# Router of a hybrid layer: experts chosen in two batches of token tiles

## The chip, the cores and the metric

One core of one Trainium2 chip runs the kernel. The metric is the device time in microseconds of one execution; lower is better. All times of instructions are microseconds from the start of the span.

## The reference, cut to what matters

One layer over 512 prompt tokens and 32 sample tokens, width 1024: a pooling branch and a differential attention are merged and projected, `x = x + merged @ w_out`, and then a mixture of experts is added. The change is in how the experts are chosen and how the token lists of each expert are made:

```
g_logits = t @ w_router_group + b_router_group          # 4 groups
g_sel = argmax(g_logits); g_w = softmax(g_logits)[g_sel]
e_logits = (t @ w_router_expert + b_router_expert)[g_sel]  # 4 experts of that group
top_v, top_i = top_k(e_logits, 2); top_w = softmax(top_v) * g_w
y += combine[:, e] * (silu(t @ w_gate[e]) * (t @ w_up[e])) @ w_down[e]     # 16 experts
```

Here `t` is the row-normalised `x`.

## The kernel before, in words

Each engine has its own queue, written out by hand; semaphores join them. Products of fp32 accuracy are made of three products of split operands (`wh`/`wl` high and low parts, in four slots), lines 1767 to 1769.

The 544 tokens are five tiles of 128 (`NT = 5`; index 0 to 4 is tile 0, 1, 2, 4, 3; the tile with the sample tokens comes fourth and is short). The output projection runs in ten steps `s`: steps 0 to 4 make the left 512 columns of the five tiles, 5 to 9 the right ones. For each step VectorE adds the result to `x` (`add_half`, lines 1485 to 1488, semaphore `o_ev`), ScalarE squares it (line 996), the tensor engine turns it (`turn_half`, line 2123), ScalarE copies the turned half (line 1003), and the tensor engine makes the half's 20 logits per token (`logits_half`, line 2131, semaphore `lg_mm`). For steps 5 to 9 ScalarE also takes the root of the row's mean square (line 1008), VectorE its reciprocal (line 1494) and the normalised rows `hb` (`normal_rows`, line 1503), which POOL sends to memory (lines 619, 621).

Logits of the left halves are copied from bank 6 into `lg`; those of the right halves are added out of bank 7, in one go for the first four tiles (lines 1527 to 1529) and apart for the last (1540, 1541). Then VectorE chooses: `first_max` (lines 1547 to 1551) three times, for the group, the first and the second expert, over all five tiles, 4 or 16 values per token, 19 chained instructions in all (each waits for the one ahead of it by `link`). `sel_done` starts 5 products on the tensor engine that count how many tokens ahead of each one chose the same expert (lines 2182, 2184), and 5 more for the totals (2188). VectorE meanwhile makes list values `oht` (1565, 1566) and the rows of the last tile, and then the place of each token in its expert's list (1570 to 1576) and one-hots over the 128 slots (`slot_hot`, 1578). Ten products make the lists (2194); line 1589 turns them into row numbers `idi`, POOL gathers the first experts' rows (595), and they are turned (2214) and split (ScalarE 1020, VectorE `xl` 1688). Behind line 1589 VectorE makes further list columns (1591), the weights (1597 to 1604), `item_w` (1609), the other list ids (1616) and `tail_lists` (1621 to 1629), which is used at the end of the kernel only. From `item_w` ten products (2281) make the weights of the slots; they stand in the tensor engine's queue directly ahead of the first expert's products.

The expert weights come in chunks of 512 KB, 24 slots `rawM`; ScalarE makes `wh` (989) and VectorE `wl` (`m_lo_split`, 1509, later 1642) of each. The first two chunks are split by VectorE between the last halves, the third after `xl`. Between its tasks in the router the tensor engine runs `idle_products`, filler that nobody reads (line 2138), in counts from the tuple `IDLE`.

The semaphores of the lists, in one line each:

```
V.tensor_tensor(ra[1][:], chosen[:, 0], chosen[:, 1], ALU.add).then_inc(sel_done, 1)
dve.wait_ge(pos_mm, 1)
```

Of the kernel before, what the change touches and what calls it, by code (L numbers as in the profile page):

```python
# [40 lines left out]
P = 128  # L41
# [69 lines left out]
def build(nc, a, o):  # L111
# [20 lines left out]
    with ExitStack() as ctx:  # L132
# [113 lines left out]
        order = r5("order", [P, NT, EXPERTS])  # L246
        assert r5.pos[0] <= 203 * K, r5.pos[0]
# [3 lines left out]
        item_hot = at("item_hot", 195 * K, [P, 2, NT, TILE_COLS, EXPERTS], F32R)  # L251
# [58 lines left out]
        norm_row = sem("norm_row")  # L310
        SUMS_IN = [32] * 4 + [48]
# [56 lines left out]
        IDLE = (3, 2, 24, 8, 5, 0, 9)  # L368
# [764 lines left out]
        def _(dve):  # L1133
# [377 lines left out]
            bc = lambda r, n: r.unsqueeze(2).broadcast_to([P, NT, n])  # L1511
# [10 lines left out]
            for i in range(NT):  # L1522
                if i == NT - 1:
                    normal_rows(i - 1)
                    dve.wait_ge(lg_mm, 2 * NT - 1)
                    early = lg[:, 0:NT - 1, :]
                    link(V.tensor_tensor(early, raw(7)[:, 0:NT - 1, :], early, ALU.add))
                    link(V.tensor_tensor(early, early, bc(rsx[:], 20)[:, 0:NT - 1, :], ALU.mult))
                    V.tensor_tensor(early, early, rb[:].unsqueeze(1).broadcast_to([P, NT - 1, 20]), ALU.add)
                add_half(NT + i)  # L1530
                if i == 0:
                    dve.wait_ge(lg_mm, NT)
                    link(V.tensor_copy(lg[:], raw(6)))
                if 1 <= i < NT - 1:
                    normal_rows(i - 1)
                if 2 <= i < 4:
                    m_lo_split(i - 2)
# [5 lines left out]
            gl, el = lg[:, :, 0:EG], lg[:, :, EG:20]  # L1543

            def first_max(src, n, m, onehot, scratch):

                link(V.tensor_reduce(m, src, AX.X, ALU.max))
                link(V.tensor_tensor(scratch, src, bc(m, n), ALU.is_equal))
                link(V.tensor_tensor(scratch, scratch, order[:, :, 0:n], ALU.mult))
                link(V.tensor_reduce(rt[:, 15, :], scratch, AX.X, ALU.min))  # L1550
                link(V.tensor_tensor(onehot, iota[:, :, 0:n], bc(rt[:, 15, :], n), ALU.is_equal))
            gmax, m1, m2 = rt[:, 0, :], rt[:, 1, :], rt[:, 2, :]
            first_max(gl, EG, gmax, ra[0][:, :, 0:EG], ra[1][:, :, 0:EG])

            link(V.tensor_scalar(ra[0][:, :, 0:EG], ra[0][:, :, 0:EG], -NEG, NEG, ALU.mult, ALU.add))
            link(V.tensor_tensor(ra[1][:].rearrange("p t (g e) -> p t g e", g=EG), el.rearrange("p t (g e) -> p t g e", g=EG),
                                 ra[0][:, :, 0:EG].unsqueeze(3).broadcast_to([P, NT, EG, EPG]), ALU.add))
            first_max(ra[1][:], EXPERTS, m1, chosen[:, 0], ra[3][:])
            link(V.scalar_tensor_tensor(out=ra[2][:], in0=chosen[:, 0], scalar=2 * NEG, in1=ra[1][:], op0=ALU.mult, op1=ALU.add))
            first_max(ra[2][:], EXPERTS, m2, chosen[:, 1], ra[3][:])  # L1560
            V.tensor_tensor(ra[1][:], chosen[:, 0], chosen[:, 1], ALU.add).then_inc(sel_done, 1)
# [15 lines left out]
            for k in range(2):  # L1577
                ins = V.tensor_tensor(slot_hot[:, k], pk[:, k].unsqueeze(2).broadcast_to([P, NT, P]),
                                      cst[:, C_SLOT:C_SLOT + P].unsqueeze(1).broadcast_to([P, NT, P]), ALU.is_equal)
                ins.then_inc(hot_done, 1)  # L1580
# [748 lines left out]
```

## Time and profile before

| what | us |
|---|---|
| median of 3 runs (lowest, highest) | 842.87 (841.27, 843.12) |
| the profiled execution, its own time | 843.01 |
| its span | 841.2 |
| tensor engine busy | 819.5 |
| VectorE busy | 589.1 |
| ScalarE busy | 512.4 |

The profile is of one execution. Its span runs from the first to the last instruction; the time of the execution holds 1.8 us more. A row of a timeline gives the start, the time of the instruction and, in brackets, the idle time of the engine ahead of it and who ended it. An instruction's pipeline end overlaps the start of the next, so steps are best counted from start to start.

### The profile page before, as it was taken

The page shows a single profiled execution, that of the slowest core. Times are in us where ns is not written, and L with a number is a line of the kernel's source. Part 1 is how long each engine was busy: PE and PEld are TensorE (multiplying, and loading weights), DVE is VectorE, ACT ScalarE, POOL GpSimd, SP SyncE. Part 2 cuts the span into 40 slices and gives each one's busy share as a digit, 9 for nine tenths or more (in the row PEclk, how much of TensorE's full clock was granted, in tenths as well). Part 3 has the DMA queues.
Part 4 walks back from the last instruction along what each step waited for, and adds up shares of the span by engine and source line. Part 5 has one row for each costly group of instructions (what it writes and reads, how often), then busy time and mean ns, then how long its engine had stood idle before and what let it go on. Part 6 is the DMA issues. An engine that isn't in the chain of part 4 may idle for free.

```text
span 841.2 us, 15813 instructions
## 1 busy us (share of the span) xinstructions
PE 819.5 (97%) x5363; PEld 747.1 (89%) x5363; DVE 589.1 (70%) x957; ACT 512.4 (61%) x935; POOL 88.4 (11%) x77
## 2 busy tenths in 40 slices
PE   9999999999999999999999999999999999999992
PEld 8999999999999998999998888888888888888881
DVE  7383233687778767466457126899989999989995
ACT  7344214567666656554634233588888888888884
POOL 0000000000000000000000001122233322223112
PEclk9999999999999999999999999999999999999997
DMA  8541222233123312332335745799999999999924
GB/s 250 123 146 57 79 68 74 68 109 89 45 81 108 86 44 92 105 99 75 101 101 195 265 165 188 254 371 376 380 375 372 364 371 365 368 366 368 345 69 192
DMA packets 135817, 163.02 MB, mean 194 GB/s; under 512 B 18584, under 2 KB 103704, under 8 KB 135772
## 3 DMA queue, kind: packets, MB, share of 16 engines
q1 hardware_dynamic: 129674, 149.53, 52.7%
q0 software_dynamic: 5952, 12.82, 5.4%
q8 instruction: 28, 0.46, 0.2%
q14 instruction: 17, 0.14, 0.1%
q10 hardware_dynamic: 146, 0.07, 0.0%
HBM read 151.09 MB, written 20.12 MB: 204 GB/s over the span
## 4 chain that ended last, share of the span: by engine, by line
PE 53%; DVE 3%; DMA 2%; issue 1%; ACT 1%; POOLq 0%; POOL 0%; ACTq 0%
PE ps L1767 15%; PE ps L1769 15%; PE ps L1768 15%; PE ps L2219 2%; PE ps L2131 1%; DMA xg<-sum_rows,idi 1%; PE ps L2138 1%; PE ps L2241 1%; DMA sum_rows<-yb,ydn 1%; PE ps L2123 0%; PE ps L2164 0%; PE ps L2165 0%; PE ps L2062 0%; DVE wl L1153 0%; PE ps L1990 0%
## 5 line engine op out<-in xcount | busy, mean ns | idle before, releaser
L1642 DVE TENSOR_TENSOR wl<-rawM,wh 128x1024 fp32r<-128x1024 f32 x189 | 223.9, 1219 | 14.4 <-ACT wh L989 14.2
L989 ACT ACTIVATE wh<-rawM 128x1024 fp32r<-128x1024 f32 x192 | 195.6, 1055 | 6.7 <-PE ps L1769 3.7
L1767 PE MATMUL ps<-hTh,wh 128*128 128x272 f32 (+2 forms) x440 | 129.2, 294 | 1.5 <-ACT qkv L813 1.0
L1769 PE MATMUL ps<-hTh,wl 128*128 128x272 f32 (+2 forms) x440 | 127.4, 290 | 0.0
L1768 PE MATMUL ps<-hTl,wh 128*128 128x272 f32 (+2 forms) x440 | 126.8, 288 | 0.0
L1767 PE MATMUL ps<-wh,xh 128*128 128x256 f32 (+1 forms) x384 | 124.7, 325 | 0.3 <-DVE xl L1688 0.3
L1769 PE MATMUL ps<-wh,xl 128*128 128x256 f32 (+1 forms) x384 | 122.0, 318 | 0.0
L1768 PE MATMUL ps<-wl,xh 128*128 128x256 f32 (+1 forms) x384 | 122.0, 318 | 0.0
L1767 PE MATMUL ps<-wh,hTh 128*128 128x384 f32 x256 | 90.0, 352 | 0.2 <-DVE mA L1273 0.2
L1769 PE MATMUL ps<-wh,hTl 128*128 128x384 f32 x256 | 86.4, 337 | 0.0
L1768 PE MATMUL ps<-wl,hTh 128*128 128x384 f32 x256 | 86.2, 337 | 0.0
L1767 PEld LDWEIGHTS ps<-hTh,wh 128*128 128x128 f32 x440 | 82.9, 189 | 3.5 <-ACT qkv L813 1.3
L1768 PEld LDWEIGHTS ps<-hTl,wh 128*128 128x128 f32 x440 | 83.1, 189 | 0.0
L1769 PEld LDWEIGHTS ps<-hTh,wl 128*128 128x128 f32 x440 | 82.9, 188 | 0.0
L1767 PEld LDWEIGHTS ps<-wh,xh 128*128 128x128 f32 x384 | 72.2, 188 | 9.9 <-issue 4.0
L1153 DVE TENSOR_TENSOR wl<-rawA,wh 128x1024 fp32r<-128x1024 f32 (+2 forms) x41 | 47.6, 1169 | 42.9 <-ACT wh L696 42.7
L1768 PEld LDWEIGHTS ps<-wl,xh 128*128 128x128 f32 x384 | 72.5, 189 | 5.7
L1769 PEld LDWEIGHTS ps<-wh,xl 128*128 128x128 f32 x384 | 72.4, 189 | 5.8
L696 ACT ACTIVATE wh<-rawA 128x1024 fp32r<-128x1024 f32 (+2 forms) x41 | 40.9, 1018 | 45.5 <-PE ps L1769 33.2
L608 POOL DMA_INDIRECT sum_rows<-yb,ydn x15 | 37.4, 2495 | 192.7 <-issue 167.4
L619 POOL DMA_DIRECT2D h_rows<-hb x4 | 2.4, 595 | 513.3 <-DVE hb L1503 513.3
L1767 PE MATMUL ps<-wh,hh 128*128 128x512 f32 x128 | 53.2, 416 | 0.6 <-DVE hl L1657 0.6
(331 smaller groups left out, 1715.0 us busy)
## 6 DMA issues: line engine op xcount, KB each, us to landing
rawM<-in_w_expert_up SPq DMA_DIRECT2D x64, 512.0 KB, 10.1
rawM<-in_w_expert_down SPq DMA_DIRECT2D x64, 512.0 KB, 8.6
rawM<-in_w_expert_gate SPq DMA_DIRECT2D x64, 512.0 KB, 9.0
rawA<-in_w_in SPq DMA_DIRECT2D x64, 192.0 KB, 3.1
rawA<-in_w_in SPq DMA_DIRECT2D x20, 512.0 KB, 5.3
rawA<-in_w_attn_branch SPq DMA_DIRECT2D x8, 512.0 KB, 3.5
rawA<-in_w_out SPq DMA_DIRECT2D x8, 512.0 KB, 4.3
x<-in_x_prompt SPq DMA_DIRECT2D x4, 512.0 KB, 6.0
```

The source lines that it names most:

```text
L608: pool.indirect_dma_start(acc_rows[:, :], bass.IndirectOffsetOnAxis(ap=ydn[:, par:par + 1], axis=0), yb[:, par, :], None, bounds_check=TOK ...
L696: nc.scalar.activation(split_slot(n)[0][:, 0:w], rawA[:, n % RA, 0:w], ACT.Copy).then_inc(hi_done, 1)
L989: nc.scalar.activation(wh[:, (c + 1) % S, :], rawM[:, slot, :], ACT.Copy).then_inc(m_hi, 1)
L1153: V.tensor_tensor(l[:, 0:w], rawA[:, n % RA, 0:w], h[:, 0:w].bitcast(F32), ALU.subtract).then_inc(lo_done, 1)
L1642: V.tensor_tensor(wl[:, sl, :], rawM[:, slot, :], wh[:, sl, :].bitcast(F32), ALU.subtract).then_inc(m_lo, 1)
L1767: T.matmul(out, sh, mh_, start=start, stop=False, **kw)
L1768: T.matmul(out, sh, ml_, start=False, stop=False, **kw)
L1769: return T.matmul(out, sl, mh_, start=False, stop=stop, **kw)
L2131: ins = T.matmul(ps[:, 6 + m, 20 * i:20 * i + 20], h2T[:, 4 * (s % 2) + k, :], wr[:, 4 * m + k, :], start=k == 0, stop=k == 3)
L2138: T.matmul(ps[:, bank, :], one, many, start=True, stop=True)
L2219: ins = T.transpose(ps[:, 2 + k // 4, P * (k % 4):P * (k % 4 + 1)], xg[:, par, P * k:P * k + P], id_m)
L2241: ins = T.transpose(ps[:, 4, P * k:P * k + P], hid[:, P * k:P * k + P], id_m)
```

## The change

The choice of experts (`finish_logits`, `select`) is made for the first three tiles before the last half of the projection is added, their places and one-hots (`place`) between that half and its logits, and for the last two tiles after the logits. The picks have a tile of their own, `picked`, and positions lie in banks 6 and 0. The products for the positions and lists are split likewise; before the logits of steps 8 and 9 the tensor engine now waits until VectorE has read the earlier ones (`lg_read`). The filler counts at the first, third and fourth place go from 3, 24, 8 to 0, 12, 3. The split of the second weight chunk moves from between the halves to behind the lists; `tail_lists` gives two instructions (`keep`) to that place and itself moves behind the third chunk's split. `item_hot` moves to the place of the squares' scratch tile, and so VectorE waits for the last square (`ach`).

```diff
+        picked = r5("picked", [P, NT, EXPERTS])
...
-        item_hot = at("item_hot", 195 * K, [P, 2, NT, TILE_COLS, EXPERTS], F32R)
+        item_hot = at("item_hot", HR + 34 * K, [P, 2, NT, TILE_COLS, EXPERTS], F32R)
...
+        lg_read = sem("logits_read")
+        AHEAD = NT - 2
...
-        IDLE = (3, 2, 24, 8, 5, 0, 9)
+        IDLE = (0, 2, 12, 3, 5, 0, 9)
...
-            for i in range(NT):
...
-                add_half(NT + i)
-                if i == 0:
-                    dve.wait_ge(lg_mm, NT)
-                    link(V.tensor_copy(lg[:], raw(6)))
-                if 1 <= i < NT - 1:
-                    normal_rows(i - 1)
-                if 2 <= i < 4:
-                    m_lo_split(i - 2)
...
+            def finish_logits(ts):
+                part, n = lg[:, ts, :], ts.stop - ts.start
+                V.tensor_tensor(part, raw(7)[:, ts, :], part, ALU.add).then_inc(lg_read, 1)
+                dve.wait_ge(lg_read, 1 if ts.start == 0 else 2)
+                link(V.tensor_tensor(part, part, bc(rsx[:, ts], 20), ALU.mult))
+                link(V.tensor_tensor(part, part, rb[:].unsqueeze(1).broadcast_to([P, n, 20]), ALU.add))
+            def first_max(ts, src, n, m, out, scratch, op=ALU.is_equal):
+                link(V.tensor_reduce(m[:, ts], src, AX.X, ALU.max))
+                link(V.tensor_tensor(scratch, src, bc(m[:, ts], n), ALU.is_equal))
+                link(V.tensor_tensor(scratch, scratch, order[:, ts, 0:n], ALU.mult))
+                link(V.tensor_reduce(rt[:, 15, ts], scratch, AX.X, ALU.min))
+                link(V.tensor_tensor(out, iota[:, ts, 0:n], bc(rt[:, 15, ts], n), op))
+            def select(ts):
+                n = ts.stop - ts.start
+                others, inside, rest, scratch = (r[:, ts, :] for r in ra)
+                first_max(ts, gl[:, ts, :], EG, gmax, others[:, :, 0:EG], scratch[:, :, 0:EG], ALU.not_equal)
+                four = lambda r: r.rearrange("p t (g e) -> p t g e", g=EG)
+                link(V.tensor_scalar(others[:, :, 0:EG], others[:, :, 0:EG], NEG, None, ALU.mult))
+                link(V.tensor_tensor(four(inside), four(el[:, ts, :]),
+                                     others[:, :, 0:EG].unsqueeze(3).broadcast_to([P, n, EG, EPG]), ALU.add))
+                first_max(ts, inside, EXPERTS, m1, chosen[:, 0, ts, :], scratch)
+                link(V.scalar_tensor_tensor(out=rest, in0=chosen[:, 0, ts, :], scalar=2 * NEG, in1=inside, op0=ALU.mult, op1=ALU.add))
+                first_max(ts, rest, EXPERTS, m2, chosen[:, 1, ts, :], scratch)
+                V.tensor_tensor(picked[:, ts, :], chosen[:, 0, ts, :], chosen[:, 1, ts, :], ALU.add).then_inc(sel_done, 1)
...
+            def list_values(ts):
+                v = values[:, :, ts]
+                V.tensor_tensor(oht[:, :, ts, TAIL:], chosen[:, :, ts, :EXPERTS - TAIL], kt(v, EXPERTS - TAIL), ALU.mult)
+                link(V.tensor_tensor(oht[:, :, ts, :TAIL], chosen[:, :, ts, EXPERTS - TAIL:], kt(v, TAIL), ALU.mult))
+            def place(ts, part):
+                n = ts.stop - ts.start
+                dve.wait_ge(pos_mm, part + 1)
+                pos = positions[part].unsqueeze(1).broadcast_to([P, 2, n, EXPERTS])
+                c, k_, j_, g_ = chosen[:, :, ts, :], pk[:, :, ts], pj[:, :, ts], ge[:, :, ts, :]
+                link(V.tensor_tensor(c, c, pos, ALU.mult))
+                link(V.tensor_reduce(k_, c, AX.X, ALU.add))
+                link(V.tensor_tensor(g_[:, :, :, 0:4], kt(k_, 4), row(C_STEP, 4, n), ALU.is_ge))
+                link(V.tensor_reduce(j_, g_[:, :, :, 0:4], AX.X, ALU.add))
+                link(V.scalar_tensor_tensor(out=k_, in0=j_, scalar=float(-P), in1=k_, op0=ALU.mult, op1=ALU.add))
+                link(V.tensor_tensor(g_, kt(j_, TILE_COLS), row(C_TILE, TILE_COLS, n), ALU.is_equal))
+                V.tensor_tensor(item_hot[:, :, ts, 0, :], kt(g_[:, :, :, 0], EXPERTS), oht[:, :, ts, :], ALU.mult)
+                for k in range(2):
+                    ins = V.tensor_tensor(slot_hot[:, k, ts, :], pk[:, k, ts].unsqueeze(2).broadcast_to([P, n, P]),
+                                          cst[:, C_SLOT:C_SLOT + P].unsqueeze(1).broadcast_to([P, n, P]), ALU.is_equal)
+                    ins.then_inc(hot_done, 1)
+            ahead, late = slice(0, AHEAD), slice(AHEAD, NT)
+            add_half(NT)
+            dve.wait_ge(lg_mm, NT)
+            link(V.tensor_copy(lg[:], raw(6)))
+            add_half(NT + 1)
+            normal_rows(0)
+            add_half(NT + 2)
+            normal_rows(1)
+            m_lo_split(0)
+            normal_rows(2)
+            add_half(NT + 3)
+            dve.wait_ge(lg_mm, NT + AHEAD)
+            finish_logits(ahead)
+            select(ahead)
+            normal_rows(AHEAD)
+            dve.wait_ge(lg_mm, 2 * NT - 1)
+            finish_logits(slice(AHEAD, NT - 1))
+            add_half(NT + 4)
+            list_values(ahead)
+            dve.wait_ge(ach, 3 * NT)
+            place(ahead, 0)
...
+            select(late)
+            list_values(late)
             normal_rows(NT - 1, scaled=True)
...
+            place(late, 1)
...
+            for part, ts in enumerate((ahead, late)):
+                ins = V.scalar_tensor_tensor(out=keep[:, ts], in0=positions[part][:, :, EXPERTS - 1], scalar=float(P),
+                                             in1=picked[:, ts, EXPERTS - 1], op0=ALU.is_lt, op1=ALU.mult)
+            link(ins)
             for k in range(2):
                 ins = V.tensor_tensor(item_hot[:, k, :, 1:, :],
                                       ge[:, k, :, 1:].unsqueeze(3).broadcast_to([P, NT, TILE_COLS - 1, EXPERTS]),
                                       oht[:, k].unsqueeze(2).broadcast_to([P, NT, TILE_COLS - 1, EXPERTS]), ALU.mult)
             ins.then_inc(hot_done, 1)
+            m_lo_split(1)
...
-                place = ps[:, 7, 0:NT * EXPERTS].rearrange("p (t e) -> p t e", t=NT)[:, :, EXPERTS - 1]
-                link(V.scalar_tensor_tensor(out=keep[:], in0=place, scalar=float(P), in1=ra[1][:, :, EXPERTS - 1],
-                                            op0=ALU.is_lt, op1=ALU.mult))
...
-            tail_lists()
...
+            tail_lists()
...
+                if s >= 2 * NT - 2:
+                    pe.wait_ge(lg_read, s - 2 * NT + 3)
...
+            pe.wait_ge(sel_done, 1)
+            T.matmul(position, tri, flat[:, es(0, AHEAD)], start=True, stop=False, **more)
+            for d in range(1, AHEAD):
+                ins = T.matmul(position[:, es(d, AHEAD)], ones, flat[:, es(0, AHEAD - d)], start=False, stop=d == AHEAD - 1, **more)
+            ins.then_inc(pos_mm, 1)
...
+            for first, last, to in ((1, 3, 0), (2, 3, 0), (0, 2, 0), (0, 1, 1)):
+                T.matmul(position_late[:, es(to, to + last - first)], ones, flat[:, es(first, last)], start=first == 1, stop=False, **more)
+            def lists(ts, part):
+                for k in range(2):
+                    pe.wait_ge(hot_done, 2 * part + k + 1)
+                    for t in range(NT)[ts]:
+                        ins = T.matmul(ps[:, 5, 0:FIRST], slot_hot[:, k, t, :], item_hot[:, k, t, 0, TAIL:],
+                                       start=(part == k == t == 0), stop=(k == 1 and t == NT - 1))
+                return ins
+            lists(slice(0, AHEAD), 0)
...
+            pe.wait_ge(sel_done, 2)
+            T.matmul(position_late, tri, flat[:, es(AHEAD, NT)], start=False, stop=False, **more)
+            T.matmul(position_late[:, es(1, 2)], ones, flat[:, es(AHEAD, NT - 1)], start=False, stop=True, **more).then_inc(pos_mm, 1)
...
+            lists(slice(AHEAD, NT), 1).then_inc(ls_mm, 1)
```

## Rows read from the trace of the kernel before

**Rows 1.** The page's table of engines: busy us, share of span, instructions.

```profile
PE 819.5 (97%) x5363; PEld 747.1 (89%) x5363; DVE 589.1 (70%) x957; ACT 512.4 (61%) x935; POOL 88.4 (11%) x77
```

**Rows 2.** The chain that ended last: start us, us, engine, what, line.

```profile
517.31 5.57 PE ps L2138 x24
...
535.46 0.50 PE ps L1767
550.06 0.87 PE ps L2219 x8
...
804.10 0.89 PE ps L2219 x8
```

**Rows 3.** The vector queue in order of time: start, us, instruction, [idle before <-releaser].

```profile
503.28 1.22 DVE L1509 TENSOR_TENSOR wl<-rawM,wh 128x1024 fp32r<-128x1024 f32 x1
506.35 0.69 DVE L1487 TENSOR_TENSOR x<-ps,x 32x512 f32<-32x512 f32 x1 [1.85 <-PE ps L2165]
...
514.15 0.69 DVE L1485 TENSOR_TENSOR x<-ps,x 128x512 f32<-128x512 f32 x1 [0.50 <-PE ps L1769]
516.47 0.16 DVE L1494 RECIPROCAL rsx<-rsx 128x1 f32<-128x1 f32 x1 [1.63 <-ACT rsx L1008]
517.42 0.18 DVE L1540 TENSOR_TENSOR lg<-ps,lg 128x20 f32<-128x20 f32 x1 [0.78 <-PE ps L2131]
...
517.91 0.18 DVE L1547 TENSOR_REDUCE rt<-lg 128x5 f32<-128x20 f32 x1
...
522.64 0.30 DVE L1565 TENSOR_TENSOR oht<-chosen,cst 128x140 f32<-128x140 f32 x1
...
523.06 1.28 DVE L1503 SCALAR_TENSOR_TENSOR hb<-x,rsx,gb 128x1024 f32<-128x1024 f32 x1
524.26 0.31 DVE L1570 TENSOR_TENSOR chosen<-chosen,ps 128x160 f32<-128x160 f32 x1
...
526.14 1.55 DVE L1578 TENSOR_TENSOR slot_hot<-pk,cst 128x640 fp32r<-128x640 f32 x2
...
528.51 0.17 DVE L1589 TENSOR_SCALAR idi<-ps 128x14 int32<-128x14 f32 x1 [0.38 <-PE ps L2194]
...
532.48 1.22 DVE L1609 SCALAR_TENSOR_TENSOR item_w<-item_hot,wgl 128x480 fp32r<-128x480 f32 x2
...
533.75 0.15 DVE L1621 SCALAR_TENSOR_TENSOR keep<-ps,ra 128x5 f32<-128x5 f32 x1
...
534.53 1.29 DVE L1688 TENSOR_TENSOR xl<-ps,xh 128x512 fp32r<-128x512 f32 x2
```

**Rows 4.** The vector queue, inside the choice of experts.

```profile
518.12 0.18 DVE L1548 TENSOR_TENSOR ra<-lg,rt 128x20 f32<-128x20 f32 x1
...
519.73 0.24 DVE L1548 TENSOR_TENSOR ra<-ra,rt 128x80 f32<-128x80 f32 x1
520.00 0.24 DVE L1549 TENSOR_TENSOR ra<-ra,order 128x80 f32<-128x80 f32 x1
```

**Rows 5.** ScalarE in order of time.

```profile
504.98 0.28 ACT L1008 ACTIVATE rsx<-ssx 128x1 f32<-128x1 f32 x1
...
515.41 0.19 ACT L996 ACTIVATION_READ_ACCUMULATOR rsq<-x 128x1 f32 x1
...
516.09 0.29 ACT L1008 ACTIVATE rsx<-ssx 128x1 f32<-128x1 f32 x1
```

**Rows 6.** Tensor engine in order of time.

```profile
527.01 1.46 PE L2194 MATMUL ps<-item_hot,slot_hot 128*128 128x14 f32 x10
...
533.81 1.33 PE L2281 MATMUL ps<-item_w,slot_hot 128*128 128x160 f32 x10
```

**Rows 7.** Transfer of the last rows to memory.

```profile
DMA to landing us min/median/max: 2.9/2.9/2.9
```

**Rows 8.** Windows of the tail: us, busy us by engine, PEclk, DMA share, GB/s.

```profile
826.00:830.00 4.00, 0.00 (x0) 0.00 (x0) 4.00 (x10) 3.95 (x11) 0.00 (x0) 1.00 0.39 132
830.00:831.00 1.00, 0.00 (x0) 0.00 (x0) 1.00 (x2) 0.31 (x2) 0.62 (x1) 0.62 0.34 135
```

More of the change, by code:

```diff
@@ L1521, in _ @@
             dve.wait_ge(gb_in, 32)
[L1522 to L1537 removed]
+            gl, el = lg[:, :, 0:EG], lg[:, :, EG:20]
@@ L1559, in _ @@
-            link(V.scalar_tensor_tensor(out=ra[2][:], in0=chosen[:, 0], scalar=2 * NEG, in1=ra[1][:], op0=ALU.mult, op1=ALU.add))
-            first_max(ra[2][:], EXPERTS, m2, chosen[:, 1], ra[3][:])
-            V.tensor_tensor(ra[1][:], chosen[:, 0], chosen[:, 1], ALU.add).then_inc(sel_done, 1)
-            kt = lambda r, n: r.unsqueeze(3).broadcast_to([P, 2, NT, n])
-            row = lambda c, n: cst[:, c:c + n].unsqueeze(1).unsqueeze(1).broadcast_to([P, 2, NT, n])
-            values = cst[:, C_LIST:C_LIST + 2 * NT].rearrange("p (k t) -> p k t", k=2)
@@ L2172, in _ @@
                     logits_half(s - 1)
+            ones, tri = cst[:, C_ONE:C_ONE + P], cst[:, C_TRI:C_TRI + P]
+            flat = picked[:].rearrange("p t e -> p (t e)")
+            position = ps[:, 6, 192:192 + AHEAD * EXPERTS]
+            position_late = ps[:, 0, 0:(NT - AHEAD) * EXPERTS]
+            es = lambda first, last: slice(first * EXPERTS, last * EXPERTS)
+            more = dict(skip_group_check=True)
+            pe.wait_ge(sel_done, 1)
[3 more added lines that the diff above has]
+            ins.then_inc(pos_mm, 1)
             idle_products(IDLE[0], 2, *chunk)
@@ L2176, in _ @@
             logits_half(2 * NT - 1)
-            idle_products(IDLE[2], 2, *chunk)
-            pe.wait_ge(sel_done, 1)
-            ones, tri = cst[:, C_ONE:C_ONE + P], cst[:, C_TRI:C_TRI + P]
-            picked = ra[1][:].rearrange("p t e -> p (t e)")
-            T.matmul(ps[:, 7, 0:NT * EXPERTS], tri, picked, start=True, stop=False, skip_group_check=True)
-            for d in range(1, NT):
-                ins = T.matmul(ps[:, 7, d * EXPERTS:NT * EXPERTS], ones, picked[:, 0:(NT - d) * EXPERTS], start=False,
-                               stop=d == NT - 1, skip_group_check=True)
@@ L2189, in _ @@
             ins.then_inc(cum_done, 1)
             idle_products(IDLE[3], 2, *chunk)
-            for k in range(2):
-                pe.wait_ge(hot_done, k + 1)
-                for t in range(NT):
-                    ins = T.matmul(ps[:, 5, 0:FIRST], slot_hot[:, k, t, :], item_hot[:, k, t, 0, TAIL:],
-                                   start=(k == t == 0), stop=(k == 1 and t == NT - 1))
-            ins.then_inc(ls_mm, 1)
+            lists(slice(AHEAD, NT), 1).then_inc(ls_mm, 1)
             idle_products(IDLE[4], 2, *slots)
-            pe.wait_ge(hot_done, 3)
+            pe.wait_ge(hot_done, 5)
```

41 lines of the change are left out of this document (9 added, 32 removed).

## The prediction

> **What bounds the kernel now.** The first view is the page's table of engines [rows 1]: the tensor engine is busy 97% of the span, so a change counts only if it moves the tensor engine's useful work. The second is the chain that ended last, in order of time [rows 2]. It runs through the tensor engine except in one place, the router between the output projection and the experts: the last logits end with the start of 24 filler products at 517.31, then come the expert lists and more filler, and the first expert product starts at 535.46. From there one expert follows the other: the hidden turn recurs from 550.06 to 804.10, 14 steps of 18.15 us, and the chain never leaves the tensor engine between them. So I treat the experts as a block that keeps its length, and the tail behind it too. The question is only by how much 535.46 moves.
>
> The filler hides what the router waits for, so the third view is the vector queue in order of time [rows 3]. From 517.42 to 535.2 it has hardly a pause: the choice of experts from 517.91, list values 522.64, normalised rows of the last tile 523.06, positions 524.26, slot one-hots 526.14, a wait for the lists until 528.51, then the list tails, the weights and `item_w`. Before 517.42 it has holes: until 514.15 it waits for the last projection (0.50), until 516.47 for a root (1.63) and until 517.42 for the logits (0.78).
>
> **Price of a vector instruction.** Chained instructions of 20 elements start 0.21 us apart (517.91 to 518.12), those of 80 elements 0.27 apart (519.73 to 520.00) [rows 3, 4]. That is 0.19 us fixed and 0.001 us per element. Two batches pay the fixed part twice. I use 0.205 us at 12 elements, 0.24 at 48, 0.20 at 8 and 0.225 at 32.
>
> **Part 1, ahead of the last projection half.** The second weight split (1.2 us, as the first one at 503.28) leaves this place. The rows of tile index 2 now come before `add_half(8)`. Their root starts on ScalarE at 504.98 [rows 5]; the vector reciprocal follows a root's start by 0.38 (516.09 to 516.47), so it starts at 505.4, the rows at 505.6, and they take 1.20 (523.06 to 524.26) to 506.8. `add_half(8)` would have been free at 506.35 and takes two pieces of 0.7: until 508.2. Three logit instructions of 60 elements at 0.25 give 509.0. `select` is 19 instructions: 6 x 0.205 + 12 x 0.24 + 0.15 for the last, whose result the queue doesn't wait for = 4.3, until 513.3. Rows of index 3, 0.2 + 1.2: 514.7. Three logit instructions of 20 elements, 0.65: 515.3. Only then comes the last `add_half`, which before started at 514.15. So it is **1.15 us late**, and what hangs on it alone too: the square, the turn and copy for the logits, the root. The turn of tile 4 and its logits stay where the projection's products put them: `add_half(8)` ends 508.2, its turn stands behind products until 509.8.
>
> **Part 2, between the last half and the last logits.** The two list values (0.37) are covered. `place(ahead)` waits for the last square, whose accumulator read starts at 515.41 and takes 0.19 in the old order [rows 5], 1.26 + 0.19 behind the add's start; with 0.1 to react it starts at 515.3 + 1.55 = 516.85. Old `place` took 3.4: seven instructions in 1.88 (524.26 to 526.14) and two one-hots of 640 elements in 1.55, of which the next instruction hides 0.1. With 3 of 5 tiles the elements fall by 64, 64, 16, 16, 4, 24 and 64, i.e. 0.25 less, and by 256 in each one-hot, 0.52 less: 2.6 us, until 519.45. The logits are there at 517.31 + 1.15 = 518.5, so they no longer decide. Reciprocal 0.2, two logit instructions 0.49 (517.42 to 517.91): the late choice starts at 520.1, **2.2 us later** than 517.91. The position products for three tiles wait for a choice done at 513.3 and are over long before; the early part of the late positions and the first list products lie in the tensor engine's free time.
>
> **Part 3, late.** `select` on two tiles: 6 x 0.20 + 12 x 0.225 + 0.15 = 4.05 against 4.73 (517.91 to 522.64), -0.68. List values -0.07. The rows stay. `place` on two tiles: seven instructions lose 96, 96, 24, 24, 6, 36 and 96 elements, -0.38, the one-hots 384 each, -0.79: together -1.17. The list's last group has 2 products instead of 5 behind the last one-hot: ten take 1.46 from 527.01 with pitches of 0.12 [rows 6], so -0.35. Sum of parts 1 to 3 at the list: 2.2 - 0.68 - 0.07 - 1.17 - 0.35 = **-0.07 us**, nothing.
>
> **Part 4, behind the list.** Two `keep` instructions (0.33, as one unchained of 0.15 at 533.75 and one chained) and the second weight split (1.2) now stand ahead of the weights and `item_w`. This stretch, 528.51 to 533.6, has no hole, so `item_w`, which ended with 533.70 (532.48 + 1.22), ends at 533.70 - 0.07 + 1.53 = 535.15. The lw products wait for it: they began at 533.81 and take 1.33 [rows 6]; now 535.2 to 536.5. The first expert product stands behind them. In the old order it had 0.32 us of slack there, being held until 535.46 by `xl`, which stood behind `tail_lists` (533.75 to 534.53). `tail_lists` now comes later, `xl` starts at 535.3 and is ready at 536.2, and the lw products decide: 536.5. The rows of the last tile, 523.06 before, start at 524.5 and reach memory about 1.6 (rows and queue) + 2.9 (landing) behind their start [rows 3, 7], at 529.0; the id list is there at 528.6, so the gather starts 0.3 late, and its turn would be at 533.2: covered by the weights. If that cover were gone it would cost 0.3. SP's only wait for the last half is the sums' transfer, and POOL asks for it behind the gathers; 1.2 us are nothing to it. The moved `tail_lists` (0.8 us) stands ahead of `lw` and of the fourth expert split, which the fourth product group needs 4.2 us behind the first (3 x 6 products of 0.23): it fits.
>
> **Sum.** 535.46 goes to 536.5: **+1.1 us**. The profiled execution took 843.01 us (span 841.2 and 1.8 around it), the median of the runs is 842.87; so by its own time it would be 844.1, by the median 842.9 + 1.1 = 844.0, which I take. Bounds: if the first batch hid altogether, part 2 would be 0 and not 2.2, `item_w` 0.75 earlier than before, and the first product at 534.3, -1.1. If two batches saved nothing of the late instructions' time (priced by the row as a whole), part 3 would be 0 but for the lists: +1.9 more, +3.0. Each instruction has a near row, so I take the middle. Changes below 0.2% (1.7 us) can't be told from none.
>
> The pitches [rows 3, 4] show 0.19 us fixed per chained instruction, at 20 elements as at 80. The Trainium skill, "VectorE: DVE Perf Modes", section "The TRN2 errata", says too that many small tiles pay a fixed cost each, but its table puts it at 58 cycles of 0.96 GHz, 0.06 us. By that estimate the first batch's 33 instructions would be some 4 us shorter and the last half not late, which is rival (a); the trace's pitch speaks against the figure.
>
> **Rivals.**
> (a) The batch hides: `add_half(9)` at 514.15 and `place(ahead)` over near the logits. For it: the holes of 0.50, 1.63 and 0.78 before 517.42 add up to 2.9 us. Against it: the moved work is 0.76 + 4.3 + 2.6 + 0.4 = 8 us and only 1.2 left. It holds if the add starts within 0.3 us of 514.15. It gives -1.1 at most, 841.8; with work I overprice behind the list too, 841.
> (b) **Slower by clock.** The filler falls from 24 + 8 + 3 products to 12 + 3 + 0, at 0.23 us each (5.57 for 24 [rows 2]). The choice takes 4.7 us from the first lists, of which 12 products cover 2.8, so the tensor engine idles about 1.5 us before 524.2, 1.1 before the late lists and 1.0 before the lw products. In the tail the granted clock was still 1.00 while the engine did nothing from 826 to 830, and fell to 0.62 and 0.50 only then [rows 8]: against. If it fell all the same to 1.2 GHz near the start of the experts, and stayed there for 3 us of products (a guess from the length of the gaps' stretch), these would take twice the time: 844.0 + 2 to 3 = 846.5. It holds if a slice between 520 and 540 shows under 1.00.
> The Trainium skill, "TensorE: Matmul & The Clock Gate", on HAM oscillation, says that gaps in the tensor engine's work bring the clock back to half; no row here shows it for gaps as short as these.
> (c) **Slower by pile-up**: `add_half(9)` 2 us late and not 1.15, because instructions with two- and three-dimensional slices cost like whole ones. It costs 1 to 1.5 more: 845.2.
> (d) The parts don't do what they say, the second split being waited for by the second product group (needed at 538): it is ready at 531, so hardly.
>
> **Numbers.** Forecast (its own range 0 to +1.7 us, all of it within 0.2%) 0.55; (a) 0.22, of which 0.12 is faster by over 0.2% and 0.10 isn't; (b) 0.08 and (c) 0.15, slower; (d) none. So faster 0.12, within 0.2% 0.65, slower 0.23. The range 842.0 to 846.0 leaves out about half of (a) and half of (b), under 0.2.
>
> **What would show it.** In the vector queue after: the last `add_half` at 515.3 with no wait ahead of it; `place(ahead)` ending near 519.4, with logits waiting for the vector engine and not the reverse; the second `sel_done` near 524.1; the 14-column ids at 528.4; the second split directly ahead of the weights; `item_w` ending 535.1; first expert product 536.5; expert period still 18.15. Wrong if the vector queue waits for the logits of the last tile, if the lw products aren't what the first expert product follows, if a clock slice falls, or if the expert period moves.

## The result: slower, by more than forecast, and spread over 4 us

The changed kernel took 846.73 us (median of 5 runs, 844.33 to 848.32), the kernel before 842.43 us (841.27 to 843.12) in the same set; the ratio is 1.005, with an interval of 1.003 to 1.007. The forecast was 844.0 (842.0 to 846.0). The profiled execution is the fastest of the five, with 844.33 us; mean granted clocks were 0.989 in it and 0.987, 0.985, 0.983 and 0.983 in the others, against 0.993 in the profile before. A second set of 12 runs (e8_after_again) gave 845.33 (843.39 to 848.72) against 842.15.

The table of engines of the page after says that the tensor engine is as busy as before (818.1 us for 819.5), and that VectorE has 34 instructions and 4.2 us more:

```profile
PE 818.1 (97%) x5351; PEld 746.5 (89%) x5351; DVE 593.3 (70%) x991; ACT 512.4 (61%) x935; POOL 88.9 (11%) x77
```

The chain that ended last, of the changed kernel, answers to [rows 2] (start us, us, engine, what, line):

```profile
536.38 0.26 PE ps L1806
...
551.11 0.87 PE ps L2273 x8
...
805.28 0.89 PE ps L2273 x8
```

The row that recurs every 18 us is the turn of the next expert's gathered rows (I had called it the hidden turn). Its 14 steps took 254.17 us, 254.04 before, so the experts kept their pace. This whole execution ran 0.93 us ahead of the old one up to the router: the last projection product is followed by other work at 513.02, in the old one at 513.95. I therefore compare a length: from there to the first turn of rows, 36.11 us before and 551.11 - 513.02 = **38.09** after. The first expert product starts at 536.22 (the chain's row 536.38 is its next step), so 23.20 behind the projection and not 21.51.

The vector queue of the changed kernel answers to [rows 3]:

```profile
508.17 0.17 DVE L1538 TENSOR_REDUCE rt<-lg 128x3 f32<-128x12 f32 x1
508.37 0.17 DVE L1539 TENSOR_TENSOR ra<-lg,rt 128x12 f32<-128x12 f32 x1
...
514.43 0.69 DVE L1488 TENSOR_TENSOR x<-ps,x 128x512 f32<-128x512 f32 x1
...
515.97 0.25 DVE L1576 TENSOR_TENSOR chosen<-chosen,ps 128x96 f32<-128x96 f32 x1 [0.61 <-DVE oht L1568]
...
519.20 0.16 DVE L1538 TENSOR_REDUCE rt<-lg 128x2 f32<-128x8 f32 x1
...
523.20 0.21 DVE L1567 TENSOR_TENSOR oht<-chosen,cst 128x56 f32<-128x56 f32 x1
...
525.60 0.22 DVE L1576 TENSOR_TENSOR chosen<-chosen,ps 128x64 f32<-128x64 f32 x1 [0.80 <-PE ps L2245]
...
528.32 0.17 DVE L1626 TENSOR_SCALAR idi<-ps 128x14 int32<-128x14 f32 x1
...
529.64 1.22 DVE L1512 TENSOR_TENSOR wl<-rawM,wh 128x1024 fp32r<-128x1024 f32 x1
...
535.03 1.28 DVE L1726 TENSOR_TENSOR xl<-ps,xh 128x512 fp32r<-128x512 f32 x2
```

Take 0.93 off my times and the vector queue's are there up to the end of the late choice. The last `add_half` starts at 514.43 (I said 515.3 - 0.93 = 514.4), `place(ahead)` at 515.97 (515.9), the late choice at 519.20 (519.2), its end at 523.20. Then comes what I hadn't: at 525.60 the queue has waited **0.80 us for the tensor engine's positions**. The tensor engine's timeline answers to [rows 6] and shows why:

```profile
515.18 0.65 PE L2162 MATMUL ps<-cst,x 128*128 128x128 f32 x4 [1.42 <-DVE x L1488]
...
520.68 4.53 PE L2179 MATMUL ps<-wl,wh 128*128 128x512 f32 x12
525.05 0.30 PE L2244 MATMUL ps<-picked,cst 128*128 128x32 f32 x2
...
535.03 1.35 PE L2335 MATMUL ps<-item_w,slot_hot 128*128 128x160 f32 x10 [0.91 <-DVE item_w L1651]
```

Twelve filler products took 4.4 us, 0.37 each, where 24 had taken 5.57 before. They end at 525.05, and the positions stand behind them, 1.7 us after the choice that they wait for was done (523.3). Windows of the new kernel and, in the second block, of the old one (busy us by engine, then the granted clock, DMA share, GB/s) give the cause:

```profile
514.00:516.00 2.00, 0.82 (x6) 0.69 (x6) 1.31 (x6) 0.84 (x3) 1.82 (x2) 1.00 0.70 230
516.00:518.00 2.00, 1.77 (x12) 1.48 (x10) 1.79 (x8) 1.98 (x4) 0.52 (x1) 0.79 0.91 308
518.00:520.00 2.00, 2.00 (x11) 2.00 (x11) 1.76 (x10) 0.90 (x1) 0.00 (x0) 0.50 1.02 323
...
522.00:524.00 2.00, 2.00 (x6) 1.52 (x6) 1.79 (x9) 0.00 (x0) 0.00 (x0) 0.50 0.36 145
524.00:526.00 2.00, 2.00 (x16) 1.79 (x14) 1.17 (x3) 0.00 (x0) 0.56 (x1) 1.00 0.00 0
```

```profile
520.00:524.00 4.00, 4.00 (x24) 3.29 (x22) 3.65 (x13) 0.00 (x0) 0.00 (x0) 1.00 0.89 320
```

The tensor engine was busy for 0.82 us of 514 to 516; from 517.2 to 524.0 it was granted half its clock, 1.2 GHz in place of 2.4. Every window of the old kernel between 500 and 560 reads 1.00.

### The profile page after: what moved, and what is told of

The parts are those of the page before. It is cut to its first block, busy times and chain, and to the rows that moved or that the text cites. A ratio compares the mean times of both kernels' runs of the same rounds, so it can differ in the third digit from the quotient of the medians.

```text
span 842.5 us, 15827 instructions
## 1 busy us (share of the span) xinstructions
PE 818.1 (97%) x5351; PEld 746.5 (89%) x5351; DVE 593.3 (70%) x991; ACT 512.4 (61%) x935; POOL 88.9 (11%) x77
## 4 chain that ended last, share of the span: by engine, by line
PE 51%; DVE 4%; DMA 2%; issue 1%; ACT 1%; POOLq 0%; POOL 0%; ACTq 0%; DVEq 0%
PE ps L1806 15%; PE ps L1808 15%; PE ps L1807 15%; PE ps L2273 2%; DMA xg<-sum_rows,idi 1%; PE ps L2172 1%; PE ps L2295 1%; DMA sum_rows<-yb,ydn 1%; PE ps L2179 1%; PE ps L2101 0%; PE ps L2162 0%; DVE wl L1156 0%; PE ps L2205 0%; PE ps L2206 0%; DVE hb L1506 0%
```

## The experiments

Two theories. **Clock**: the thinner work on the tensor engine in the router lets the clock fall, at varying places; then filler takes double time, and filler stands ahead of the positions, the lists and the gathered rows. **Vector queue**: the work moved ahead of the last half and the split moved behind the lists cost all of it. The lengths below are those of the one profiled execution, the times medians. The length is not all of the time: among the 13 profiles the experts' 14 steps take 253.4 to 254.6 us, and what follows the last turn of rows, which I call the tail, 36.8 to 38.3 (37.1 before).

| kernel | us (lowest, highest) | before, same runs | ratio | projection to first turn of rows |
|---|---|---|---|---|
| before | | | | 36.11 |
| changed | 846.73 (844.33, 848.32) | 842.43 | 1.005 [1.003, 1.007] | 38.09 |
| e1_fill | 846.36 (845.47, 847.6) | 842.62 | 1.0037 [1.0024, 1.0051] | 40.06 |
| e2_before_thin | 846.24 (846.01, 846.93) | 842.62 | 1.0041 [1.0028, 1.0055] | 40.95 |
| e3_split_alone | 843.47 (842.84, 844.6) | 842.62 | 1.0008 [0.9999, 1.0017] | 37.17 |
| e4_rows_behind | 845.41 (844.3, 846.82) | 842.62 | 1.0031 [1.0022, 1.0041] | 37.45 |
| e5_full_fill | 843.81 (842.99, 847.84) | 842.15 | 1.0025 [1.0013, 1.0037] | 37.87 |
| e6_best | 844.78 (843.42, 845.59) | 842.15 | 1.0026 [1.0015, 1.0036] | 36.69 |
| e7_no_fill | 845.17 (844.44, 846.3) | 842.15 | 1.0033 [1.0021, 1.0044] | 39.55 |
| e8_after_again | 845.33 (843.39, 848.72) | 842.15 | 1.0032 [1.0016, 1.0048] | 39.42 |
| e9_order2 | 843.37 (842.06, 844.78) | 842.18 | 1.0014 [1.0005, 1.0022] | 36.77 |
| e10_fill_fit | 844.5 (843.02, 845.94) | 842.18 | 1.0024 [1.0015, 1.0032] | 40.21 |
| e11_rows_fill | 843.5 (842.43, 846.28) | 842.18 | 1.0021 [1.0012, 1.003] | 37.25 |

**e2_before_thin: the filler alone, in the old order.**

```diff
-        IDLE = (3, 2, 24, 8, 5, 0, 9)
+        IDLE = (0, 2, 12, 3, 5, 0, 9)
```

> The kernel before with the changed kernel's filler counts (0, 2, 12, 3 for 3, 2, 24, 8) and nothing else. The vector queue is untouched. Theory 1 (the clock): holes of some 0.8, 0.6 and 2.8 us open between 514 and 523, the clock falls to 0.50 in the router or the first expert, and the time rises by 1 to 4 us, to 843.5 to 846.5, spread over that. Theory 2: filler is read by nobody and the time stays at 842.4.

It took 3.6 us more. This is the old kernel, nothing but products that nobody reads left out, and it is as slow as the change. The tensor engine's timeline and the windows of 5 us:

```profile
516.25 2.99 PE L2138 MATMUL ps<-wl,wh 128*128 128x512 f32 x12
521.85 0.45 PE L2182 MATMUL ps<-ra,cst 128*128 128x80 f32 x2 [2.62 <-DVE ra L1561]
...
532.51 4.19 PE L2138 MATMUL ps<-slot_hot 128*128 128x512 f32 x9
```

```profile
525.00:530.00 5.00, 4.32 (x15) 3.62 (x15) 3.67 (x13) 1.71 (x3) 0.43 (x1) 0.50 0.22 91
530.00:535.00 5.00, 5.00 (x18) 4.32 (x17) 4.18 (x16) 0.00 (x0) 1.67 (x2) 0.50 0.53 151
535.00:540.00 5.00, 5.00 (x26) 4.38 (x26) 1.69 (x3) 2.14 (x3) 0.53 (x2) 0.69 0.96 311
```

The tensor engine waited 2.62 us for the choice, and the clock was 0.50 from 524.5 to 538.1. At 0.50 the nine fillers of the last group took 4.2 us for 2.3, and the gathered rows were turned at 536.49, 23.5 us behind the projection's end and not 19.1. That is the clock theory's first support, and it shows that rival (b) needs no batches. The length grew by 4.8 us, the median by 3.6.

**e8_after_again: the changed kernel once more.**

> The changed kernel unaltered, for a second profile and more times. The profiled execution was its fastest (844.3, one fall of the clock, 517 to 524, mean clock 0.989), the others took 846.5 to 848.3 at 0.983 to 0.987. Theory 1: median 846.5, and a profile at or over 846 shows a second stretch at 0.50 between 527 and 541, with the fillers there taking double and the first expert product 2 us later; a profile near 844.3 shows one stretch alone. Theory 2: the slower executions differ elsewhere, and the router's stretch looks alike in both profiles.

The profile is of an execution of 847.01 us, and theory 1 had its mark: two stretches at 0.50, 519.7 to 523.1 and 530.0 to 536.8.

```profile
520.00:525.00 5.00, 5.00 (x23) 4.07 (x21) 4.38 (x21) 0.00 (x0) 0.00 (x0) 0.69 0.69 235
...
530.00:535.00 5.00, 5.00 (x16) 4.02 (x16) 4.25 (x14) 0.00 (x0) 2.41 (x2) 0.50 0.36 96
535.00:540.00 5.00, 5.00 (x29) 4.59 (x28) 3.06 (x8) 2.69 (x4) 1.97 (x2) 0.82 0.95 293
```

```profile
531.00 4.19 PE L2179 MATMUL ps<-slot_hot 128*128 128x512 f32 x9
534.99 1.91 PE L2268 MATMUL ps<-cst,xg 128*128 128x128 f32 x8
...
537.82 0.44 PE L1806 MATMUL ps<-wh,xh 128*128 128x512 f32 x1
```

The first expert product is 24.33 behind the projection, 1.1 later than in the profile with one fall (I had said 2). The first fall cost the vector queue nothing here, as it found the positions ready; the second doubled the filler ahead of the gathered rows. So the same kernel has executions with one fall and with two. Of the 2.6 us between the two spans the router's length is 1.3, the tail 1.0 (38.2 for 37.2) and the stage ahead of the router 0.5. Over the 12 executions time and clock go together: the five at 0.988 to 0.990 took 843.4 to 844.8, the six at 0.982 to 0.985 took 845.3 to 848.7, and the one at 0.987 is the profiled one.

**e1_fill: one gap filled.**

```diff
-        IDLE = (0, 2, 12, 3, 5, 0, 9)
+        IDLE = (6, 2, 12, 3, 5, 0, 9)
```

> The changed kernel with six filler products instead of none in the gap in which the tensor engine waits for the last add_half (IDLE first entry 0 to 6). Theory 1 (the clock): that gap, 1.42 us behind the small position products, is what makes the granted clock fall to 0.50 from 517 to 524 in the changed kernel; filled, the clock stays at 1.00 there, the 12 fillers behind the first lists take 2.8 us and not 4.5, the vector engine no longer waits 0.8 us for the late positions, and the time is 842.4 + 1.0 = 843.5, with little spread between runs. Theory 2 (vector queue alone: the work moved ahead and the split behind the lists cost it all): the filler changes nothing, 846.7 with the same spread.

This miss taught the most. I had put the fall down to the 1.42 us gap ahead of 515.18; filled, the time stayed at 846.4, and the clock fell twice, 519.5 to 526.3 and 529.7 to 536.6:

```profile
514.65 1.64 PE L2179 MATMUL ps<-wl,wh 128*128 128x512 f32 x6
516.22 0.66 PE L2162 MATMUL ps<-cst,x 128*128 128x128 f32 x4
...
517.57 1.07 PE L2172 MATMUL ps<-wr,h2T 128*128 128x20 f32 x8 [0.22 <-ACT h2T L1006]
518.48 1.04 PE L2231 MATMUL ps<-picked,cst 128*128 128x32 f32 x8
519.38 1.32 PE L2238 MATMUL ps<-item_hot,slot_hot 128*128 128x14 f32 x6
520.55 5.47 PE L2179 MATMUL ps<-wl,wh 128*128 128x512 f32 x12
```

From the projection to the fall this queue has no gap over 0.22 us, and from 500 to 517 it is busy throughout at 1.00. What it did between the projection and the fall was six instructions for the positions, six fillers, four turns, two fillers, eight logit instructions, eight more for the positions and the first for the lists. So this fall had no gap of note ahead of it, and filling the largest gap isn't enough. The length, 40.06, is above both profiles of the change (38.09, 39.42); the 12 fillers took 5.5 us of it.

**e5_full_fill and e10_fill_fit: filler as thick as before, all through.** The four extra products stood between the turn of the gathered rows and the lw products; e10_fill_fit leaves those four out.

```diff
-        IDLE = (0, 2, 12, 3, 5, 0, 9)
+        IDLE = (6, 2, 18, 7, 6, 0, 9)
...
+            idle_products(2, 2, *chunk)
             lists(slice(0, AHEAD), 0)
...
             gathered(0, 0, 0)
+            idle_products(4, 7, *slots)
             pe.wait_ge(wgt_done, 1)
```

> The changed kernel with every gap of the tensor engine in the router filled by 512-column products: counts 6, 2, 18, 7, 6, 9, two more ahead of the first list products and four more between the turn of the gathered rows and the lw products (54 in all; before had 51, the change 31). Theory 1 (what counts for the clock is the share of wide products, not whether the engine is busy: with six fillers in one gap alone the clock still fell): the clock stays at 1.00 from 514 to 540 and the time is 842.5 + 1.0 = 843.5 with a spread under 2 us. If it fell once more, the double time of the fillers is in the way and it is 846 or more. Theory 2 (vector queue alone): no better than the changed kernel, 846.7.

> The changed kernel with the filler counts 6, 2, 18, 7, 6, 9 and two more, without the four ahead of the lw products, which stood 0.8 us in their way in the fully filled version. The vector queue is exactly the change's. This is the change's own price with the clock held: by the prediction's sum +1.05, so 842.2 + 1.0 = 843.2 and clock 1.00 in all of 514 to 540. By the rival that the vector queue alone cost the 3 to 4 us: 845.3.

In the profile of e5_full_fill the clock is 1.00 throughout, and the vector queue shows the change's own price:

```profile
514.45 0.69 DVE L1488 TENSOR_TENSOR x<-ps,x 128x512 f32<-128x512 f32 x1
...
524.74 0.21 DVE L1576 TENSOR_TENSOR chosen<-chosen,ps 128x64 f32<-128x64 f32 x1
...
527.44 0.17 DVE L1626 TENSOR_SCALAR idi<-ps 128x14 int32<-128x14 f32 x1
...
528.76 1.22 DVE L1512 TENSOR_TENSOR wl<-rawM,wh 128x1024 fp32r<-128x1024 f32 x1
...
532.71 1.22 DVE L1651 SCALAR_TENSOR_TENSOR item_w<-item_hot,wgl 128x480 fp32r<-128x480 f32 x2
...
534.61 0.69 DVE L1726 TENSOR_TENSOR xl<-ps,xh 128x512 fp32r<-128x512 f32 x1 [0.55 <-ACT xh L1023]
```

The wait for the positions is gone (524.74). The ids are at 527.44, 14.40 behind the projection's end, 14.56 before: -0.16, my sum said -0.07. `item_w` ends at 533.93, 20.89 behind, 19.75 before: **+1.14**. The extra fillers then held the lw products (those that read `item_w`) until 535.14 (my own doing), `xl` at 534.6 would have allowed 535.5, about 1.0 later than before. That `xl` waited 0.55 us, and not for the vector queue: the gathered rows came late.

```profile
528.97 1.97 POOL L598 DMA_INDIRECT xg<-h_rows,idi  x1 [3.29 <-DMA h_rows<-hb]
...
533.29 1.09 PE L2269 MATMUL ps<-cst,xg 128*128 128x128 f32 x8 [0.95 <-DMA xg<-h_rows,idi]
```

POOL waited for the last rows to reach memory, as forecast, and began the gather 0.24 us later than before, counted from the projection (0.3 forecast). But from there to the turn it took 4.3 us and not 3.4, and the gather's first instruction 1.97 us where it had taken 1.08. So the turn began 20.25 behind the projection, before 19.06, and the weights no longer covered it. That instruction took 2.0 to 2.1 us in five profiles (e3_split_alone, in the old order, among them, and e4_rows_behind, e5_full_fill, e8_after_again, e11_rows_fill) and 1.1 to 1.2 in the other eight; why isn't shown.

Ten of 12 runs lie between 842.99 and 844.98; the other two, 846.61 and 847.84, have the lowest clocks, 0.989.

e10_fill_fit has its median, 844.5, between its two figures (843.2 and 845.3). Of 11 runs five took 843.0 to 843.9 at clocks 0.991 to 0.994, the rest 844.5 to 845.9. The three at 0.989 and 0.990 all took 845.4 or more, and the profile is one of them:

```profile
520.00:525.00 5.00, 5.00 (x14) 3.94 (x14) 4.14 (x17) 0.00 (x0) 0.07 (x1) 0.50 0.51 198
```

```profile
520.13 6.71 PE L2179 MATMUL ps<-wl,wh 128*128 128x512 f32 x18
526.68 0.30 PE L2245 MATMUL ps<-picked,cst 128*128 128x32 f32 x2
```

The clock was 0.50 from 518.3 to 525.2. The 18 fillers took 6.7 us, and the positions began at 526.68, counted from the projection 3.2 us later than in e5_full_fill. Up to 518 this queue had done the same as e5_full_fill's, where nothing fell. So more filler makes a fall rarer (the mean clock is 0.991 or more in 10 of e5_full_fill's 12 executions and in 8 of e10_fill_fit's 11, in none of the change's 17) and not impossible. What theory 1 for e5_full_fill says counts for the clock isn't shown by any run here. A fall is dearer with thicker filler: 3.2 us at this point, against 1.4 for the change's 12 on the same count.

**e7_no_fill: no filler at all.**

```diff
-        IDLE = (0, 2, 12, 3, 5, 0, 9)
+        IDLE = (0, 0, 0, 0, 0, 0, 0)
```

> The changed kernel with no filler product at all in the router. It tells where a low clock costs: if mainly through the filler itself, which at 0.50 takes 0.46 us each and stands in the way of the positions, lists and gathered rows, the time falls to 844 or 845 though the clock is low for longer; if mainly through the experts' first products at half rate, it is 847 or more (the clock low from 517 until some us behind the first expert product, each us of product there costing one). By the vector queue alone it would be 846.7.

```profile
520.00:525.00 5.00, 3.06 (x16) 2.97 (x15) 4.45 (x20) 0.00 (x0) 0.00 (x0) 0.50 0.52 197
...
535.00:540.00 5.00, 5.00 (x18) 4.34 (x18) 4.01 (x10) 1.36 (x3) 2.12 (x3) 0.52 0.94 283
```

845.17, within 1.9 us, at a mean clock of 0.977 to 0.982: the clock is low from 515.9 to 539.8, three times as long as in the first profile of the change, and yet the time is no worse than the change's 845.33 on that chip. The first product starts at 536.77, 23.63 behind the projection, and about 3 us of the experts' products run at half rate, +1.4. The router's own loss is about 1.1 us, against the 22.5 that e5_full_fill would have allowed. It is mostly the lw products, which the experts wait for: they take 2.42 us here and 1.33 in the kernel before. So half clock costs little where the vector queue decides. It costs in the lw products and the first expert's products and, where there is filler, through filler in the way.

**e3_split_alone: part 4 alone, in the old order.**

```diff
-                if 2 <= i < 4:
-                    m_lo_split(i - 2)
+                if i == 2:
+                    m_lo_split(0)
...
             ins.then_inc(hot_done, 1)
+            m_lo_split(1)
             dve.wait_ge(ge_done, 1)
```

> The kernel before with only the second weight split moved from between the last halves to behind the lists; tail_lists and keep stay where they were. The prediction's part 4: item_w ends 1.2 us later (about 534.9), the lw products start then and the first expert product at about 536.3 instead of 535.46; 842.4 + 0.8 to 1.2 = 843.4, clock as before. If the clock theory bites here too (the tensor engine has a hole of about 1.1 us ahead of the lw products), a slice under 1.00 shows and the time is over 845. If the split hides in the vector queue, 842.4.

843.47, +0.85, clock as before. Its vector queue, where the first stage ran 0.97 us ahead of the old profile's:

```profile
527.53 0.17 DVE L1589 TENSOR_SCALAR idi<-ps 128x14 int32<-128x14 f32 x1 [0.38 <-PE ps L2195]
...
528.59 1.22 DVE L1509 TENSOR_TENSOR wl<-rawM,wh 128x1024 fp32r<-128x1024 f32 x1
...
532.54 1.22 DVE L1610 SCALAR_TENSOR_TENSOR item_w<-item_hot,wgl 128x480 fp32r<-128x480 f32 x2
...
534.61 1.29 DVE L1689 TENSOR_TENSOR xl<-ps,xh 128x512 fp32r<-128x512 f32 x2
```

The split takes 1.14 to the next start and shifts all that follows it in the vector queue: `item_w` ends 1.03 us later than before. The length is 37.17, 1.06 more than before, but it can't separate the split from another cause: the gathered rows came late in this profile, as in e5_full_fill (turn 20.31 behind the projection, before 19.06), and `xl` needs them too: in e5_full_fill, where ScalarE began its part of them at the same 533.98, `xl` started at 534.61 as well. The two causes fall together here. The median, +0.85, is the better measure of the split.

**e4_rows_behind and e11_rows_fill: the last `add_half` on time.** The second has the fitted filler too.

```diff
-            normal_rows(AHEAD)
+            row_scale(AHEAD)
             dve.wait_ge(lg_mm, 2 * NT - 1)
             finish_logits(slice(AHEAD, NT - 1))
             add_half(NT + 4)
             list_values(ahead)
+            normal_rows(AHEAD, scaled=True)
```

> The changed kernel with the normalised rows of tile index 3 made behind the last add_half and its list values, where the vector queue otherwise waits 0.6 us for the last square; only the 0.2 us reciprocal stays ahead. The last add_half should then start within 0.1 us of the end of the projection instead of 1.2 us behind it, and the tensor engine's wait of 1.42 us shrinks to about 0.3. Theory 1 (the clock): it stays at 1.00, the late choice starts 0.6 us earlier, and the time is 842.4 + 0.4 = 842.8. Theory 2 (no part of the clock): 846.7 - 0.6 = 846.1.

> The changed kernel with the rows of tile index 3 behind the last add_half and filler 3, 2, 18, 7, 6, 9 and two more. With thin filler this order still had two falls of the clock, 519 to 523 and 529 to 533, and 845.4. With the clock held it is the vector queue's price of the late add_half alone: the late choice 0.6 us earlier than in the version with fitted filler, 842.2 + 0.4 = 842.6. If the lateness cost nothing, equal to that version, 843.2.

e4_rows_behind took 845.41, between my two figures: the clock still fell, 519.2 to 522.6 and 529.5 to 532.9, with the wait for the last half down to 0.28 us. With filler (e11_rows_fill) the clock of the profile stayed at 1.00, and the ids come 13.89 behind the projection, 14.40 in e5_full_fill:

```profile
526.90 0.17 DVE L1627 TENSOR_SCALAR idi<-ps 128x14 int32<-128x14 f32 x1
```

So the lateness of `add_half` is worth 0.5 us at the ids (I had said 0.6). The median is 843.5 and I had said 842.6; the runs spread up to 846.28. The profiled one, 844.76, shows what else there is with the clock held: of the 1.8 us by which its span exceeds the old one's, the router's length is 1.1, the experts' steps 0.4 and the tail 1.2 (in it the last gather of sums took 9.3 us for 8.2), and it was 0.9 ahead up to the router.

**e6_best and e9_order2: the costs taken out.** Both are made from e11_rows_fill. e6_best has `keep` and `tail_lists` ahead of `xl`, as in the old order, and the second split behind `xl`. e9_order2 moves only the second split, to just ahead of `xl`; that is the edit shown.

```diff
-            m_lo_split(1)
             dve.wait_ge(ge_done, 1)
...
+            m_lo_split(1)
             dve.sem_inc(hid_done, 1)
```

> Batches as changed, with the three costs that the profile shows taken out: the rows of tile index 3 behind the last add_half, the second weight split behind xl (ahead of the third), keep and tail_lists ahead of xl as in the old order, and filler counts 3, 2, 18, 7, 6, 9 with two more ahead of the first lists. Theory 1: the last add_half on time, late choice 0.7 us earlier than in the changed kernel, item_w 1.5 us earlier than there, first expert product bound by the gathered rows at about 0.3 us ahead of the old kernel's; clock 1.00; 842.5 - 0.3 = 842.2, the same as before within the noise. If batching itself gained what its name says, it would be 841 or less; if the clock falls all the same, 845.

> As the version before it (batches kept, rows of index 3 behind the last add_half, filler 3, 2, 18, 7, 6, 9 and two more), but only the second weight split stands ahead of xl, in the 1.0 us in which the vector queue there waits for ScalarE, keep stays where the change has it and tail_lists behind the third split. The fourth product group should no longer wait for its split (0.6 us before). First expert product about 0.2 us ahead of the old kernel's, counted from the end of the projection; clock 1.00; 842.2 + 0 = 842.2 (841.5 to 843). If splitting the choice gained anything that can be measured once its costs are gone, it is 841 or less.

e6_best, with 844.78, missed its forecast of 842.2 and lost what it won: its first expert product came 21.07 behind the projection, before 21.51, but the first expert then waited 0.60 us for its weight split, which the split behind `xl` had pushed back. Its length is 0.6 more than before; the experts' steps (254.58 us) and the tail (37.9) were long in its profile too, but both are within what other profiles show. e9_order2 is the best of the batched versions, 843.37 (forecast 842.2), ratio 1.0014 [1.0005, 1.0022]. Its profile (842.20 us) has the first expert product at 21.61 and a length of 36.77, 0.66 more than before. No batched version beats the kernel before: with most of its costs taken out the batching gains nothing, and the best one is still slower by a little.

## Why the prediction was wrong

**Right**: the vector queue's sum. Part 1 (last half 1.15 us late: 1.2), part 2 (late choice at 519.2 by this profile's clock: 519.20), part 3 (-0.07 at the ids: -0.16 in e5_full_fill), part 4 (`item_w` +1.45: +1.14 in e5_full_fill; +1.03 for the split alone in e3_split_alone). For the first expert product the sum said +1.1, and e5_full_fill would have allowed about +1.0. The times fit it less well than the queue: e5_full_fill's median is +1.7, 0.7 of it by its own four fillers, and e10_fill_fit's is +2.3. Its five quickest executions, 843.0 to 843.9 over 842.18, are where the sum puts them, but whether the clock held in them isn't on record. One step of the sum held only in part: the gathered rows were to be covered by the weights. In the profiles of the change and of e10_fill_fit they were, in those of e5_full_fill and e11_rows_fill `xl` waited for them.

**Wrong**: the sum has no term for the clock. It adds up the vector queue and the lw products alone and puts the loss of 20 filler products at nothing; the old kernel with that filler alone took 3.6 us more (e2_before_thin). I had this as rival (b), slower by clock, gave it 0.08, and it is what happened. Three steps in it failed.

- "Against" stood on [rows 8]: at the end of the kernel the clock stayed at 1.00 for 4 us of nothing. One such stretch doesn't bound the rule. In the change the clock fell 2.0 us behind a gap of 1.42, and in e1_fill with no gap over 0.22 behind the projection. The old trace held no example of thin work, so the row couldn't speak for or against, and the chance should have been near one half.
- I counted the filler as cover and its loss as holes (1.5 + 1.1 + 1.0 us; the first, given as 4.7 less 2.8, comes to 1.9). But a hole in which the vector queue decides costs nothing. What the loss costs is the clock: e2_before_thin takes 3.6 us more by that alone.
- I priced a fall by the experts' first products, 2 to 3 us. In the profile after they ran at 1.00, in that without filler half clock cost 1.4 there. The fall costs through filler, which is a fixed number of products and doubles: 12 fillers 4.4 us and not 2.8, so the positions 1.7 us late, of which the vector queue felt 0.80; in e8_after_again nine fillers 4.2 us and not 2.3.

The Trainium skill, "TensorE: Matmul & The Clock Gate", on HAM oscillation, warned of gaps between bursts; the trace agrees on the direction (0.50 for some 7 us in the first profile after, with a gap of 1.42 us ahead of it), and e1_fill adds a fall without such a gap. The figure of the Trainium skill, "VectorE: DVE Perf Modes", section "The TRN2 errata", by which rival (a) would have come (58 cycles, 0.06 us), did not hold: the 12-element instructions of the changed kernel start 0.20 us apart (508.17 to 508.37).

Rival (c), pile-up, was wrong: the late start was 1.2 us as reckoned. Rival (a) too: nothing hid.

**Open**: what in the work of the tensor engine sets off a fall, why one program falls in some runs and not in others, and what separates the slower runs at 0.991 to 0.993 in e10_fill_fit and e11_rows_fill (up to 846.1 in the latter) from the rest. Only the profiled execution of each set shows its stretches. The profiles name two candidates outside the clock, the first gather and the tail, each worth up to about 1 us. The old kernel has such runs too: 846.05 us at 0.993 in one set of 27.

## What to carry to other kernels

Filler products are part of a latency-bound stage: whoever reorders it has to look at the granted clock microsecond by microsecond, and ask of each filler whether at half rate it still ends before the work that stands behind it is due. Part of the filler was no better than none here (845.33 and 845.17). Work moved off the end of a chain gains only where the same engine idles: here 8 us of vector work went to a place with 2.9 us of holes, and 33 short instructions paid their fixed 0.19 us a second time. Where the clock hangs on chance, one profile is not enough: the fastest of five looked like the forecast.

## What the runs showed of the hardware that I had not expected

- The clock fell although the tensor engine's queue had had no gap over 0.22 us in the 5.4 us since the projection (e1_fill; small products and eight fillers in that time).
- It fell for about 7 us at a time in the profiles of the change and e1_fill (517.2 to 524.0, 519.5 to 526.3, 529.7 to 536.6) and for less in others (519.2 to 522.6 and 529.5 to 532.9 in e4_rows_behind).
- The kernel without any filler in the router, 24 us at half clock, took 845.17 us, less than the changed kernel's first set and as much as its second.
- The same gather instruction on POOL took 1.1 to 1.2 us in eight profiles and 2.0 to 2.1 in five.
